# The first feed-forward product with W1 tiles stationary and u moving, in a decoder layer on one Trainium2 core

## What is computed

```python
# D_MODEL = 2048, SEQ = 256, D_FF = 8192
u = x * (1 + scale2) + shift2
h = jnp.square(jax.nn.relu(u @ w_ff1[l]))
x = layer_norm(DEEPNORM_ALPHA * x + gate2 * (h @ w_ff2[l]), ln2_g[l], ln2_b[l])
```

## Time and profile before

| | |
|---|---|
| median of 3 runs | 3045.56 us (3043.03 to 3046.35) |
| span of the profiled execution | 3039.8 us |
| its own time | not shown beside the span; the median is 5.8 us above the span |
| PE busy | 2797.1 us, 92% of the span |
| loads of stationary tiles (PEld) | 2316.4 us, 76% |
| DVE busy | 1873.8 us, 62% |
| ACT busy | 1280.3 us, 42% |
| feed-forward stage | from some 2290 us to 3018 us of the span |

### The profile page before, as it was taken

The page is one execution under the profiler, slowest core; times in us unless marked ns, Lnnn a source line. Parts: engine busy times, 40 slices in busy tenths (PEclk is TensorE's granted clock), DMA queues, the critical chain, the costliest instruction groups (busy, mean ns, idle before and its releaser), DMA issues. The chain is left out here.

```text
span 3039.8 us, 44529 instructions
## 1 busy us (share of the span) xinstructions
PE 2797.1 (92%) x13932; PEld 2316.4 (76%) x13932; DVE 1873.8 (62%) x2418; ACT 1280.3 (42%) x1644; POOL 292.4 (10%) x231
## 2 busy tenths in 40 slices
PE   1299999999999999999999999999988999999997
PEld 1277887787877878778787888888776888888885
DVE  6876666776667676676765455455566554555555
ACT  0145325543345433463344444443444444344443
POOL 1002131031210322003310000000002000000000
PEclk6589999999999999999999999999998999999998
DMA  8765454754447544574535566656544556565555
GB/s 279 251 200 174 126 146 133 229 160 135 136 143 231 148 147 125 178 216 140 162 116 169 188 190 188 198 187 190 204 159 134 187 185 187 187 185 187 186 187 173
DMA packets 277445, 535.45 MB, mean 176 GB/s; under 512 B 20865, under 2 KB 21249, under 8 KB 275969
## 3 DMA queue, kind: packets, MB, share of 16 engines
q1 hardware_dynamic: 270928, 523.83, 55.6%
q10 hardware_dynamic: 6320, 9.32, 0.8%
HBM read 530.98 MB, written 2.10 MB: 175 GB/s over the span
## 5 line engine op out<-in xcount | busy, mean ns | idle before, releaser
L956 DVE TENSOR_TENSOR w_lo<-raw,w_hi 128x1024 fp32r<-128x1024 f32 x803 | 1009.3, 1257 | 736.5 <-ACT w_hi L567 679.0
L567 ACT ACTIVATE w_hi<-raw 128x1024 fp32r<-128x1024 f32 x803 | 848.6, 1059 | 1125.1 <-PE acc L1429 823.6
L1429 PE MATMUL acc<-w_hi,u_hi 128*128 128x512 f32 x2176 | 886.7, 408 | 26.3 <-DVE w_lo L956 15.0
L1429 PE MATMUL acc<-w_hi,u_lo 128*128 128x512 f32 x2176 | 859.1, 395 | 0.0
L1429 PE MATMUL acc<-w_lo,u_hi 128*128 128x512 f32 x2176 | 859.0, 395 | 0.0
L1429 PEld LDWEIGHTS acc<-w_hi,u_hi 128*128 128x128 f32 x2176 | 416.0, 191 | 117.4 <-issue 18.5
L1429 PEld LDWEIGHTS acc<-w_hi,u_lo 128*128 128x128 f32 x2176 | 415.0, 191 | 90.5
L1429 PEld LDWEIGHTS acc<-w_lo,u_hi 128*128 128x128 f32 x2176 | 415.9, 191 | 79.8 <-issue 1.0
L1429 PE MATMUL acc<-w_hi,z_hi 128*128 128x512 f32 x1024 | 404.8, 395 | 0.0
L1429 PE MATMUL acc<-w_lo,z_hi 128*128 128x512 f32 x1024 | 404.3, 395 | 0.0
L1429 PE MATMUL acc<-w_hi,z_lo 128*128 128x512 f32 x1024 | 404.3, 395 | 0.0
(11 more groups left out here) (236 smaller groups left out, 2066.6 us busy)
## 6 DMA issues: line engine op xcount, KB each, us to landing
raw<-in_w_in SPq DMA_DIRECT2D x416, 512.0 KB, 3.9
raw<-in_w_ff SPq DMA_DIRECT2D x259, 512.0 KB, 4.2
raw<-in_w_ada SPq DMA_DIRECT2D x192, 512.0 KB, 4.5
raw<-in_w_branch_a SPq DMA_DIRECT2D x32, 512.0 KB, 4.0
raw<-in_w_branch_b SPq DMA_DIRECT2D x32, 512.0 KB, 4.3
raw<-in_w_branch_c SPq DMA_DIRECT2D x32, 512.0 KB, 4.3
raw<-in_w_o SPq DMA_DIRECT2D x32, 512.0 KB, 4.3
x_sb<-in_x ACTq DMA_DIRECT2D x1, 2048.0 KB, 9.3
```

The source lines that it names most:

```text
L567: a.activation(w_hi[:, u % PARTS, :, :], raw[:, rl % RAWS, :, :], ACT.Copy).then_inc(hi_ready.sem, 1)
L956: v.tensor_tensor(w_lo[:, u % PARTS, :, :], raw[:, rl % RAWS, :, :], w_hi[:, u % PARTS, :, :], ALU.subtract).then_inc(lo_ready.sem, 1)
L1429: return t_.matmul(dst, lhsT, rhs, start=start, stop=stop)
```

## The change

The first product no longer goes through `k_tile` but through a new function, `k_tile_cols`. For each of the BPC = 4 blocks of 128 weight columns, the W1 tile is stationary and the 256 tokens of u move, three matmuls each. The result in `acc` has hidden channels on the partitions and tokens along the free dimension, block b in columns b*256 to b*256 + 255 of the flattened accumulator, which is the layout that the second product wants. Two blocks share a bank of PSUM, and only the first of them starts its accumulation with the start flag. PE's transposes of `stage` and their semaphore `h_turned` are gone. ACT makes `z_hi` from `stage` in one instruction, directly after the square, with no step of the weight stream between them; DVE makes `z_lo` from `stage`. The relu of a job waits for the `z_lo` of the job before.

```diff
@@ ACT, feed-forward
                     if j:
-                        act.wait_ge(N["h_turned"].sem, N["h_turned"].value(i, j))
+                        act.wait_ge(N["h_lo"].sem, N["h_lo"].value(i, 2 * j))
...
                     activate(stage[:, :, :], stage[:, :, :], ACT.Square, "squared", j + 1)
-                    next_slot(3)
-                    act.wait_ge(N["h_turned"].sem, N["h_turned"].value(i, j + 1))
-                    for h in range(2):
-                        activate(z_hi[:, 4 * j + 2 * h:4 * j + 2 * h + 2, :],
-                                 bank[2 * (j % 2) + h][:, :].rearrange("p (a b) -> p a b", a=2), ACT.Copy,
-                                 *(("h_hi", j + 1) if h else ()))
+                    next_slot()
+                    act.wait_ge(N["squared"].sem, N["squared"].value(i, j + 1))
+                    activate(z_hi[:, 4 * j:4 * j + 4, :].rearrange("p a b -> p (a b)"), flat(stage), ACT.Copy, "h_hi", j + 1)
@@ DVE, feed-forward
                     for h in range(2):
-                        tt(z_lo[:, 4 * j + 2 * h:4 * j + 2 * h + 2, :].rearrange("p a b -> p (a b)"), bank[2 * (j % 2) + h][:, :],
+                        tt(z_lo[:, 4 * j + 2 * h:4 * j + 2 * h + 2, :].rearrange("p a b -> p (a b)"), stage[:, h, :],
                            z_hi[:, 4 * j + 2 * h:4 * j + 2 * h + 2, :].rearrange("p a b -> p (a b)"), ALU.subtract, "h_lo", 2 * j + h + 1)
@@ PE
+            def k_tile_cols(n, u, q, dst, j, right):
+                k = UK * (u % UPJ) + q
+                hi, lo = right
+                if q == 0:
+                    pe.wait_ge(lo_ready.sem, n + 1)
+                if k == 0:
+                    pe.wait_ge(acc_free[dst].sem, j)
+                sl = u % PARTS
+                for b in range(BPC):
+                    bs = slice(b * P, (b + 1) * P)
+                    out_ = acc[dst][:, b // 2, (b % 2) * S:(b % 2 + 1) * S]
+                    t_.matmul(out_, w_hi[:, sl, q, bs], hi[:, k, :], start=k == 0 and b % 2 == 0, stop=False,
+                              skip_group_check=True)
+                    t_.matmul(out_, w_hi[:, sl, q, bs], lo[:, k, :], start=False, stop=False, skip_group_check=True)
+                    last = t_.matmul(out_, w_lo[:, sl, q, bs], hi[:, k, :], start=False, stop=k == KT - 1,
+                                     skip_group_check=True)
+                if q == UK - 1:
+                    last.then_inc(units_used.sem, 1)
@@ PE, slots
-                        k_tile(i * units + (unit0 + s // 2), s // 2, s % 2, job % 2,
+                        (k_tile_cols if job < cols else k_tile)(i * units + (unit0 + s // 2), s // 2, s % 2, job % 2,
@@ PE, feed-forward
-                next_slot = slots(i, FF_JOBS * UPJ, J_FF * UPJ, count, ff_left)
-                for j in range(FF_JOBS):
-                    while count[0] < (j + 1) * KT:
-                        next_slot()
-                    if j < NCH:
-                        next_slot(2)
-                        pe.wait_ge(N["squared"].sem, N["squared"].value(i, j + 1))
-                        for b in range(BPC):
-                            for m in range(MT):
-                                last = turn(bank[2 * (j % 2) + b // 2][:, (b % 2) * S + m * P:(b % 2) * S + (m + 1) * P],
-                                            stage[:, m, b * P:(b + 1) * P])
-                        last.then_inc(N["h_turned"].sem, 1)
+                next_slot = slots(i, FF_JOBS * UPJ, J_FF * UPJ, count, ff_left, NCH)
+                while count[0] < FF_JOBS * KT:
+                    next_slot()
```

More of the change, by code:

```diff
@@ L320, in layer_program @@
                 merged_made=1, ln_scaled=1, xhat_made=1, xhat_turned=1, u2_even=1, u2_odd=1, u2_hi=1, u2_lo=1,
-                base_made=1, squared=NCH, h_turned=NCH, h_hi=NCH, h_lo=UPJ).items():
+                base_made=1, squared=NCH, h_hi=NCH, h_lo=UPJ).items():
             N[name] = signal(name, per)
@@ L1450, in k_tile, with slots @@
                     last.then_inc(units_used.sem, 1)
-            def slots(i, units, unit0, count, left):
+            def k_tile_cols(n, u, q, dst, j, right):
[16 more added lines that the diff above has]
+                    last.then_inc(units_used.sem, 1)
+            def slots(i, units, unit0, count, left, cols=0):
                 def one():
```

## The result

In one comparison the changed kernel took 3051.6 us (median of 13 executions, 3044.14 to 3057.38) against 3043.03 for the kernel before (13, 3036.66 to 3049.15). The ratio is 1.0025, with an interval from 1.0014 to 1.0035: by the ratio 7.6 us slower, between 4.3 and 10.7; the two medians differ by 8.6. The forecast was +4.7 us and 3050.

The account below looks back on a forecast made before the run. PE was taken to bound the kernel, through its matmul count and pitch. Terms of -14.2, +19.9 and -1.0 made +4.7 us on a span of 3039.8, and 5.8 us of distance gave 3050, range 3024 to 3075.

Parts of the forecast that it names:

- Term 2: First product on PE: 3072 matmuls of 256 columns at 120.0 ns each against 113.3, +20.5 us, +19.9 after covered k-tiles.
- The 20 ns of z: Second product, z stationary: 20 ns above the stream per matmul, giving an upper bound of 126.7 ns for the new matmuls.
- The second rival: First product: load and stream collide, pitch 121 to 130 ns; at 126.7, +24.8 us and 3070 us; chance 0.17.
- The first rival: First product: extra time goes with the columns or vanishes, pitch 109 to 116 ns; 3030 or 3017 us; chance 0.34.
- A load's record as occupancy: First product: each load occupies PE for its recorded 188 ns, 2256 ns per k-tile, +229 us; chance 0.02.
- Term 1: PE's transposes go: 0.89 us saved per first-product job, 16 jobs, -14.2 us.
- Term 3: Second product: without transposes the pitch may return from 233.3 to 232.1 ns, -1.9 us; half taken, -1.
- PE idle within the stage: Sign in the feed-forward stage's profile after that would make the prediction wrong; no size given.
- ACT's cover: After a job, w_hi starts 1.06 us later but 2.7 us of cover remains; failing it, 3066 us, chance 0.05.

Follow-up runs that it names:

- e2: Changed kernel with only 64 of each block's 128 weight columns stationary in the first product, half of h not computed; 3024.93 us in one execution.
- e5: e1 with only 64 of each block's 128 tokens of u stationary in the first product, 512 columns of w moving; 3036.98 us in one execution.
- b1: Kernel before with z and what shares its region moved up by 640 bytes; 3026.16 us, ratio 0.9938.
- e6: Changed kernel with u_hi and all behind it moved up by 384 bytes; 3038.99 us, ratio 0.9985.
- e3: Changed kernel with only 128 of the 256 tokens moving in the first product, loads whole, half of h not computed; 3097.81 us in one execution.
- e1: Changed kernel with the old first product (u stationary, 512 columns of w moving), still without transposes; 3027.94 us, ratio 0.995.
- e4: Kernel before with PE's feed-forward loop of four passes written as two passes of two quarters each; 3039.29 us in one execution.
- a1: Changed kernel with z moved up by 640 bytes, as in b1; 3034.24 us, ratio 0.996.
- c3: c2 with z and what shares its region moved up by 640 bytes; 3027.46 us, ratio 0.9938.
- c4: c3 with z moved up by 384 bytes in place of 640; 3021.52 us, ratio 0.9921.
- c2: Changed kernel with u_hi and u_lo joined, 512 columns moving past one w_hi and 256 of u_hi past w_lo; 3033.9 us, ratio 0.9975.

## Why the prediction was right

**How near the numbers are.** The 3050 of the forecast stands 1.6 us from the 3051.6 measured, closer than the reasoning deserves: its base of 3045.56 was 2.5 us above the 3043.03 that before has in the comparison, and the change was forecast at +4.7 where it came out at +7.6 by the ratio.

**Term 2, the pace, right.** The step was "it belongs to a matmul and its load, it stays whole: 120.0", from rows 8 against rows 4. Measured 120.0, and the first products grew by 9.2 us where term 2 less the twelve groups of transposes that stand there makes 19.9 - 10.7 = 9.2. The reason held in part: the load takes part, since half of it gave 113.3 at 256 columns (e2). But half of it gave 229.6 and not 220.0 at 512 (e5), and at a granted clock of 0.50 nothing stands on top of the stream at either length. So that the very 13.3 of 512 columns came back whole at 256 is measured, and why is not shown; e2 and the floor of some 112 ns leave room for a cost by columns (6.7) plus a meeting of load and stream at 256. In this the forecast had some luck. The reasoning was too simple in another point, too. The 20 ns of z that I took as upper bound are no dearer load as such but 13.3 plus 6 for the place of the tile (b1, e6). The second rival was built on that bound, and at u's and w's places it had nothing to rest on; still it was right to give it a chance, as the trace of before could not tell place from load.

**The first rival (113.3 or less) fell.** 113.3 ns appeared only with half the load (e2), and the floor of loads at some 112 only when the stream was 53 ns (e3). The Trainium skill (TensorE: Matmul & The Clock Gate, "Back-to-back issue gap") has 262 cycles (109 ns) for 256 columns as the gap of a matmul by itself, by which a gain of 28 us was worked out; for streams of load and matmul pairs it gives 81 ns with 128 columns and 131 with 512. The traces have 120.0, 111.7 (e3) and 226.7, and a loss, so none of these figures holds for this stream of loads and matmuls.

**A load's record as occupancy fell** as forecast: the group of loads by form has 194 ns each, and they start 120 ns apart.

```profile
L1463 PEld LDWEIGHTS acc<-u_hi,w_hi 128*128 128x128 f32 x1024 | 198.5, 194 | 12.6 <-DVE w_lo L953 10.4 <-issue 2.2
```

**Term 1, right.** -14.2 forecast; the pieces of e1 give -14.6, and its time has -15.3 for terms 1 and 3 together.

**Term 3, sized a little low.** The second product runs at 232.4 ns in place of 233.3 and not at 232.1 in full. Its pieces lost 3.5 us. The four groups of transposes in them are -3.6 and the gaps at three jumps +1.4, so -1.4 us is left for the pace; I took -1. The reason given, that the transposes bring the 233.3, is not borne out in full: in e5, without transposes, the second products of quarters 2 to 4 took 89.59 us each, which is 233.3, and in e4, with them, the one of the first quarter ran at the other pace. (Two sums of the prediction are off by 0.1 us and change nothing: 1536 x 1.2 is 1.8, 96 x 13.4 is 1.3.)

**The missing term.** "PE idle within the stage" was on my list of what would make the prediction wrong, and it happened, at +1.4 us: the loop's body went from 800 to 1152 matmuls and no longer runs without fetches. I had costed the doubled instructions as time on PE and not as bytes that PE has to fetch. With it the sum is 4.7 + 1.4 - 0.4 = +5.7, the stage's figure in the two profiles, in the lower part of the measured interval (4.3 to 10.7). With the 2.4 us that the gaps cost in a1 it would be +6.7.

**ACT's cover held.** The timelines of ACT and then DVE after a job, as in the earlier trace rows:

```profile
2397.30 1.03 ACT L913 ACTIVATE stage<-acc 128x1024 f32<-128x1024 f32 x1 [1.90 <-PE acc L1466]
2398.36 1.06 ACT L561 ACTIVATE stage<-stage 128x1024 f32<-128x1024 f32 x1
2399.45 1.06 ACT L561 ACTIVATE z_hi<-stage 128x1024 fp32r<-128x1024 f32 x1
2400.41 1.99 ACT L567 ACTIVATE w_hi<-raw 128x1024 fp32r<-128x1024 f32 x2
...
2401.49 1.22 DVE L953 TENSOR_TENSOR w_lo<-raw,w_hi 128x1024 fp32r<-128x1024 f32 x1 [4.83 <-ACT w_hi L567]
```

z_hi took 1.06 us; w_lo was ready at 2402.71, 5.4 us after relu began, as worked out. DVE's longest wait grew from 3.5 to 4.8 us, and none of it reached PE.

## What to carry to other kernels

Swapping stationary and moving operands to save transposes is paid in loads: if the moving side gets shorter, there are more matmuls, and here each brought 13.3 ns even where its load hides in the stream, so count the pairs and not the columns; where two streams share a stationary tile, move them past it together. Before changing an algorithm for a few microseconds, compare the pace of like matmuls with different stationary tensors: 6 ns between two of them was the tiles' start address, worth 18 us for a changed offset, where the whole change moved 8. And count the instructions of an unrolled loop body, since they are fetched again on each pass once they are too many.

## What the runs showed of the hardware

- The pace of a load and matmul pair depends on where the tiles lie. On a 512-byte grid, with stationary tiles 384 bytes beyond the moving w, the pace was 232.4 ns for 512 columns (z in the changed kernel, u in e6); with stationary tiles at the place of w, or 256 beyond, 226.7 (b1, e6). With half loads at u's good place it was 229.6 (e5). The law behind it, and the two paces of c3 and c4, stay open.
- At a granted clock of 0.50 the same matmuls start 426.7 ns (512 columns, before) and 213.3 ns (256 columns, changed kernel) apart, twice the stream with nothing on top; at 1.00 both have 13.3 ns on top of it.
- A row of matmuls of 128 columns or fewer with a full load each has a pace of 109 to 112 ns at a granted clock of 1.00 (e3).
- The granted clock of 0.50 lasted through the 169.55 us of the first quarter's first product in e3, with 128 columns moving. With 256 columns, in the changed kernel, it was back at 1.00 some 4 us after the wait for w_lo ended, as with 512 before.
- A loop body of 896 matmuls or more had its instructions fetched on every pass, with steps of 0.5 to 1.4 us at most jumps back (after, c2, c4, e4); bodies of up to 800 had none (before, e1).
